# Seven block products in place of eight for the FFN output products of a two-layer decoder trunk

## The reference

```python
def swiglu(h, w_in, w_out):
    gu = h @ w_in                              # (512, 1024) @ (1024, 5632)
    g, u = jnp.split(gu, [FFN_HIDDEN], axis=-1)     # FFN_HIDDEN = 2816
    return (jax.nn.silu(g) * u) @ w_out        # (512, 2816) @ (2816, 1024)

    for layer in range(DEPTH):
        ...
        x = x + rms_norm(m, norm_mix_post[layer])
        hn = rms_norm(x, norm_ffn_pre[layer])
        x = x + rms_norm(swiglu(hn, ffn_w_in[layer], ffn_w_out[layer]), norm_ffn_post[layer])
```

## Time and profile before

| what | us |
|---|---|
| median of three runs | 1206.71 |
| span of the profiled execution | 1204.9 |
| TensorE busy | 1193.1 |
| GpSimd (POOL) busy | 517.1 |
| ScalarE (ACT) busy | 398.4 |
| VectorE (DVE) busy | 321.0 |

### The profile page before, as it was taken

The page is one execution under the profiler, slowest core; times in us unless marked ns, Lnnn a source line. Parts: engine busy times, 40 slices in busy tenths (PEclk is TensorE's granted clock), DMA queues, the critical chain, the costliest instruction groups (busy, mean ns, idle before and its releaser), DMA issues.

```text
span 1204.9 us, 14579 instructions
## 1 busy us (share of the span) xinstructions
PE 1193.1 (99%) x5566; PEld 988.6 (82%) x5566; DVE 321.0 (27%) x553; ACT 398.4 (33%) x623; POOL 517.1 (43%) x288
## 2 busy tenths in 40 slices
PE   7999999999999999999999999999999999999998
PEld 6888887898888888888888888788888888888886
DVE  3351056251011111000056835825211111110002
ACT  5112336453233323222243324634433323331210
POOL 4546431744444344444427433033644344435330
PEclk9999999999999999999999999999999999999999
DMA  7454303243232323222443352022332323223211
GB/s 269 128 127 138 105 2 104 72 140 106 87 104 87 104 89 103 92 101 97 159 147 129 98 163 83 18 70 88 106 105 87 104 90 102 94 98 99 94 53 70
DMA packets 34648, 123.82 MB, mean 103 GB/s; under 512 B 3715, under 2 KB 3971, under 8 KB 34348
## 3 DMA queue, kind: packets, MB, share of 16 engines
q1 hardware_dynamic: 30328, 109.94, 27.0%
q10 hardware_dynamic: 4276, 13.26, 3.8%
HBM read 119.76 MB, written 3.42 MB: 102 GB/s over the span
## 4 chain that ended last, share of the span: by engine, by line
PE 99%; DMA 0%; DVE 0%; ACT 0%; DVEq 0%; POOLq 0%; issue 0%; POOL 0%
PE ps L1053 30%; PE ps L1055 30%; PE ps L1054 30%; PE ps L1260 2%; PE ps L1226 2%; PE ps L1083 1%; PE ps L1244 1%; DMA ident<-ident_in 0%; PE ps L1272 0%; PE ps L1362 0%; PE ps L1340 0%; PE ps L1224 0%; PE ps L1352 0%; PE ps L1365 0%; PE ps L1223 0%; PE ps L1378 0%
## 5 line engine op out<-in xcount | busy, mean ns | idle before, releaser
L279 POOL TENSOR_TENSOR w_lo<-w_raw,w_hi 128x1024 fp32r<-128x1024 f32 x199 | 477.0, 2412 | 560.7 <-ACT w_hi L387 559.1
L1053 PE MATMUL ps<-h_hi,w_hi 128*128 128x512 f32 (+1 forms) x1008 | 383.7, 381 | 0.0
L1055 PE MATMUL ps<-h_hi,w_lo 128*128 128x512 f32 (+1 forms) x1008 | 382.3, 379 | 0.0
L1054 PE MATMUL ps<-h_lo,w_hi 128*128 128x512 f32 (+1 forms) x1008 | 382.2, 379 | 0.0
L387 ACT ACTIVATE w_hi<-w_raw 128x1024 fp32r<-128x1024 f32 x200 | 209.4, 1056 | 304.4 <-DMA w_raw<-weights 301.9
L1053 PEld LDWEIGHTS ps<-h_hi,w_hi 128*128 128x128 f32 x1008 | 189.6, 188 | 35.9 <-issue 0.5
L1054 PEld LDWEIGHTS ps<-h_lo,w_hi 128*128 128x128 f32 x1008 | 189.7, 188 | 35.5 <-issue 0.2
L1055 PEld LDWEIGHTS ps<-h_hi,w_lo 128*128 128x128 f32 x1008 | 189.6, 188 | 35.5
L1053 PE MATMUL ps<-w_hi,prod_hi 128*128 128x512 f32 x352 | 137.2, 390 | 0.0
L1055 PE MATMUL ps<-w_hi,prod_lo 128*128 128x512 f32 x352 | 137.0, 389 | 0.0
L1054 PE MATMUL ps<-w_lo,prod_hi 128*128 128x512 f32 x352 | 137.0, 389 | 0.0
(11 more groups left out here) (126 smaller groups left out, 758.2 us busy)
## 6 DMA issues: line engine op xcount, KB each, us to landing
w_raw<-weights SPq DMA_DIRECT2D x200, 512.0 KB, 3.3
x<-x_in SPq DMA_DIRECT2D x4, 512.0 KB, 7.1
gain_post<-norms ACTq DMA_DIRECT2D x4, 512.0 KB, 4.0
gate_w_a<-gate_rows ACTq DMA_DIRECT2D x1, 2048.0 KB, 7.1
minus_f<-forget_rows ACTq DMA_DIRECT2D x1, 2048.0 KB, 11.5
gain_pre<-norms ACTq DMA_DIRECT2D x3, 512.0 KB, 4.2
gate_w_b<-gate_rows ACTq DMA_DIRECT2D x1, 1536.0 KB, 10.7
out<-x SPq DMA_DIRECT2D x3, 512.0 KB, 2.6
```

The costliest lines, as they stand in the source:

```text
L279: nc.gpsimd.tensor_tensor(w_lo[:, c % RING], w_raw[:, c % RING], w_hi[:, c % RING].bitcast(F32), ALU.subtract).then_inc(lo_done, 1)
L1053: mm(to, held[0], moved[0], start=start, stop=False)
L1054: mm(to, held[0], moved[1], start=False, stop=False)
L1055: return mm(to, held[1], moved[0], start=False, stop=stop)
```

## The change

The output product is cut in two by two blocks: tokens in halves of 256, hidden units in halves of 11 tiles, output columns in halves of 512. Strassen's identity (in its form with shared sums) gives the four blocks of the result from seven block products. Three of them take a block of the output weights as it is (`W11`, `W22`, `W21`), four take differences of weights (`T1` to `T4`). A product has six chunks, the sixth of half width, so an FFN's output stage has 42 chunks of 12 (or 6) matmuls.

- **Weight differences ("folds").** During the gate and up stage SyncE loads four weight blocks in six pieces into a buffer `stage`, VectorE makes the four differences there (`fold`), SyncE stores them to a DRAM tensor `fold_t`, from which the ring loads them later. Load and store of a piece stand between the ring's loads on SyncE's queue, which is written out in full instead of a loop.
- **Sides.** VectorE makes sums and differences of the activations (`sides`) for pairs 11 to 21; ScalarE and VectorE split each of the six sides in three pieces (`split`).
- **Merging.** Products that enter several blocks are added by VectorE (`merge`) or accumulated on a bank that holds an earlier product.
- **The boundary after layer 0.** Tiles 0 and 1 are complete after product 5, tile 2 within product 6, tile 3 at its end. GpSimd makes the low parts of V1 and V1+1 ahead of its boundary steps and those of V1+2 and V1+3 between them.
- The low parts of the weights are GpSimd's as before, of half width for a sixth chunk.

```diff
-V1 = FOUT0 + FT
+V1 = FOUT0 + 7 * 6
...
+PRODUCTS = ((False, W11), (True, T2), (True, T1), (True, T3), (False, W22), (True, T4), (False, W21))
+PIECES = ((0, 4), (4, 8), (8, FH))
+FOLDS = 6
...
-            groups = N_CHUNKS // RING
-            with nc.sync.Fori(1, groups) as g:
-                for i in range(RING):
-
-                    sp.wait_ge(chunk_used, g * RING + (i + 1 - RING))
-                    sp.dma_start(w_raw[:, i], weights[g * RING + i]).then_inc(raw_landed[i], 16)
...
+            for c in range(AHEAD, N_CHUNKS):
+                if c >= RING:
+                    sp.wait_ge(chunk_used, c + 1 - RING)
+                at = fout(c)
...
+                    if folded_t:
+                        sp.wait_ge(fold_stored, 16 * FOLDS * (layer + 1))
...
+                sp.dma_start(w_raw[:, c % RING, 0:width(c)], source).then_inc(raw_landed[c % RING], 16)
+                for layer in range(2):
+                    j, late = divmod(c - FINS[layer] - 6, 4)
+                    if 0 <= j < FOLDS and late in (0, 2):
+                        part = slice(j * CHUNK, min((j + 1) * CHUNK, FH * SEQ))
+                        held = stage[:, :, 0:part.stop - part.start]
+                        if late == 0:
+
+                            if FOLDS * layer + j:
+                                sp.wait_ge(fold_stored, 16 * (FOLDS * layer + j))
+                            sp.dma_start(held, fold_w[layer].rearrange("b p k -> p b k")[:, :, part]).then_inc(fold_landed, 16)
+                        else:
+                            sp.wait_ge(folded, FOLDS * layer + j + 1)
+                            sp.dma_start(fold_t.ap()[layer].rearrange("b p k -> p b k")[:, :, part], held).then_inc(fold_stored, 16)
...
                 for t in range(1, TILES):
+                    if b == 2 and t <= 2:
+                        low(AFTER[b] + t + 1)
                     post_rstds(b, t)
                     pre_rstds(b, t)
...
+            for c in range(FOUT0 + 6, V1 + 2):
+                low(c)
+            boundary(2)
...
+                act.wait_ge(sides_done, FH * (layer + 1))
+                act.wait_ge(chunk_used, c0)
+                split(0)
+                highs(c0 + 6, c0 + 8)
+                split(1)
+                highs(c0 + 8, c0 + 12)
+                act.wait_ge(chunk_used, c0 + 6)
...
+                split(2)
+                highs(c0 + 12, c0 + 18)
+                split(3)
+                highs(c0 + 18, c0 + 24)
+                act.wait_ge(chunk_used, c0 + 12)
+                split(4)
+                split(5)
+                highs(c0 + 24, c0 + 32)
...
+            act.wait_ge(chunk_used, FOUT0 + 36)
             act.dma_start(gate_w[0][:], gate_rows[0:4].partition_broadcast(P)).then_inc(gate_w_landed[0], 16)
...
+            def fold(layer, j):
+
+                n = min(CHUNK, FH * SEQ - j * CHUNK)
+                w11, w12, w21, w22 = (stage[:, i, 0:n] for i in range(4))
+                vec.wait_ge(fold_landed, 16 * (FOLDS * layer + j + 1))
+                own(nc.vector.tensor_tensor(w11, w12, w11, ALU.subtract))
+                nc.vector.tensor_tensor(w12, w22, w12, ALU.subtract)
+                own(nc.vector.tensor_tensor(w22, w22, w11, ALU.subtract))
+                nc.vector.tensor_tensor(w21, w21, w22, ALU.subtract).then_inc(folded, 1)
...
+                nc.vector.tensor_tensor(s1, a21, a22, ALU.add)
+                own(nc.vector.tensor_tensor(a21, a11, a21, ALU.subtract))
+                own(nc.vector.tensor_tensor(a11, s1, a11, ALU.subtract))
+                nc.vector.tensor_tensor(s4, a12, a11, ALU.subtract).then_inc(sides_done, 1)
...
+                for p in range(FT):
+                    if p % 2 == 0 and p // 2 < FOLDS:
+                        fold(layer, p // 2)
+                    if p == FH:
+
+                        vec.wait_ge(fold_stored, 16 * FOLDS * (layer + 1))
+                    vec.wait_ge(silu_done, tile0 + p + 1)
...
+                def split(n):
+                    raw, hi, lo = SIDES[n]
+                    for i, (k0, k1) in enumerate(PIECES):
+                        vec.wait_ge(side_hi, len(PIECES) * (len(SIDES) * layer + n) + i + 1)
+                        nc.vector.tensor_tensor(lo[:, k0:k1, :], raw[:, k0:k1, :], hi[:, k0:k1, :].bitcast(F32),
+                                                ALU.subtract).then_inc(side_ready, 1)
...
+                product(0, (4, 6), False, first_ready)
+                product(1, (0, 2), False, side(0))
+                pe.wait_ge(product_done, FT * (layer + 1))
+                product(2, (5, 7), False, side(1))
...
+                for i in range(3):
+                    chunk(6, i, (4, 6), True, side(5)).then_inc(chunk_used, 1)
+                for t in range(2):
+                    if b < 4:
+                        turn(b, t)
+                    for i in range(3, 6):
+                        last = chunk(6, i, (4, 6), True, side(5), (t,))
```

More of the change, by code:

```diff
@@ L365, in _ @@
                 nc.gpsimd.tensor_tensor(y, y, ret_gate[:, :, h * HEAD:(h + 1) * HEAD], ALU.mult).then_inc(ret_y, 1)
-            at = OUT0 + 3
-            for b in range(1, 4):
-                lows(at, AFTER[b] + AHEAD - 1)
-                boundary(b)
-                at = AFTER[b] + AHEAD
-            lows(at, N_CHUNKS)
+            lows(OUT0 + 3, AFTER[1] + AHEAD - 1)
+            boundary(1)
+            lows(FIN0 + AHEAD, FOUT0)
+            lows(FOUT0, FOUT0 + 6)
+            for c in range(FOUT0 + 6, V1 + 2):
+                low(c)
+            boundary(2)
+            lows(V1 + AHEAD, AFTER[3] + AHEAD - 1)
+            boundary(3)
+            lows(FIN1 + AHEAD, FOUT1)
+            lows(FOUT1, FOUT1 + 6)
+            for c in range(FOUT1 + 6, N_CHUNKS):
+                low(c)
             boundary(4)
@@ L696, in own, with half_scale @@
                 vec.wait_ge(vec_step, steps[0])
-            def half_scale(b):
-                for t in range(TILES):
+            def half_scale(b, tiles=range(TILES)):
+                for t in tiles:
+                    bank = half_bank(b, t)
                     vec.wait_ge(half_summed, 4 * (b - 1) + t + 1)
@@ new lines, in halves_of, with ffn_out, split, merge @@
+            def halves_of(row, n=SEQ):
+                return row.rearrange("p (a s) -> p a s", s=n)
+            def ffn_out(layer):
+                c0, b = FOUTS[layer], 2 * layer + 2
+                def split(n):
+                    raw, hi, lo = SIDES[n]
+                    for i, (k0, k1) in enumerate(PIECES):
+                        vec.wait_ge(side_hi, len(PIECES) * (len(SIDES) * layer + n) + i + 1)
+                        nc.vector.tensor_tensor(lo[:, k0:k1, :], raw[:, k0:k1, :], hi[:, k0:k1, :].bitcast(F32),
+                                                ALU.subtract).then_inc(side_ready, 1)
+                def merge(to, bank, held):
+                    nc.vector.tensor_tensor(to, ps[:, bank, :], held, ALU.add).then_inc(merged, 1)
+                split(0)
+                split(1)
+                split(2)
+                for t in range(2):
+                    vec.wait_ge(chunk_used, c0 + 12)
+                    vec.wait_ge(first_copied, 2 * layer + t + 1)
+                    merge(work[:, t, :], 2 * t, work[:, t, :])
+                split(3)
+                for t in range(2):
+                    vec.wait_ge(chunk_used, c0 + 18)
+                    vec.wait_ge(merged, 10 * layer + t + 1)
+                    merge(work[:, 2 + t, :], 5 + 2 * t, work[:, t, :])
+                split(4)
+                split(5)
+                for t in range(2):
+                    vec.wait_ge(chunk_used, c0 + 24)
+                    vec.wait_ge(merged, 10 * layer + 2 + t + 1)
+                    merge(ps[:, 1 + 2 * t, :], 2 * t, work[:, 2 + t, :])
+                half_scale(b, (0, 1))
+                for t in range(2):
+                    vec.wait_ge(chunk_used, c0 + 30)
+                    merge(ps[:, 5 + 2 * t, :], 5 + 2 * t, work[:, t, :])
+                half_scale(b, (2, 3))
+                for t in range(2):
+                    vec.wait_ge(chunk_used, c0 + 36)
+                    merge(ps[:, 2 * t, :], 2 * t, work[:, t, :])
@@ L941, in _ @@
             boundary(1)
[L942 removed]
+            ffn(0)
+            ffn_out(0)
             boundary(2)
[L945 to L946 removed]
             def dots(n0, n1):
```

292 lines of the change are left out of this document (186 added, 106 removed).

## The result

The changed kernel takes 1214.1 us, median of four runs (1212.3 to 1215.2); the kernel before, on the same chip, 1206.8. The ratio is 1.006, with an interval of 1.0048 to 1.0072: slower by 7.3 us, by 0.6%. The forecast of 1206.9 was 7.2 us too low; the time lies between its own upper end (1212) and the slower rival (1227), in the interval that the prediction gave to folds that are too slow (above 1212, chance 0.33). The profiled execution of the changed kernel is the fastest of the four: 1212.3 us, span 1210.4, 5.5 more than the span before.

A forecast was written before the change was run, and what follows sets the result against it. TensorE, busy 99% of the span, was taken as the bound. From 1206.7 us, -29.9 (matmuls) + 4.8 (low parts) + 13.5 (end of layer 0) + 11.8 (folds) = +0.2: 1206.9, own range 1202 to 1212, eight in ten 1185 to 1230.

The forecast's parts named there:

- Matmuls: Output products of both layers: 462 instead of 528 matmuls a layer, at 0.226 us each, 29.9 us less.
- Low parts late: Output products: GpSimd, taking turns with VectorE, reaches product 4's first chunk late; TensorE waits 2.4 us a layer, 4.8 together.
- E: End of a layer's up products, the zero from which the prediction counted times in the output stage.
- End of layer 0: Layer 0's last output products: TensorE waits 9.7 us to turn tile 0 and 3.8 for tile 1, together 13.5.
- Folds: Gate and up stages: late weight differences hold up TensorE, 5.9 us a layer, 11.8 together, range 0 to 32.
- The clock: Gate and up stages: the first fold's 3.8 us wait may end in slow matmuls, 1.0 us (0 to 2.5).
- The pauses for the product: Gate and up stages: TensorE waits 3.8 us at the first fold, 1.0 at the second, 0 to 0.5 at later ones.
- Port costs little: GpSimd hardly held up, differences hidden, only 8.6 us at layer 0's end stay: 1185 us; chance with a halfway case 0.32.
- Folds don't fit the period: Gate and up stages: slow transfers of 6.2 us make a 24.2 us cycle, some 16 us a layer: 1227; chance 0.33.
- It doesn't do what it says: Rival doubting the matmul saving; dismissed because seven products with the same 512 columns are fewer matmuls; no chance given.
- Covers costed at nothing: Gate-row loads, VectorE's wait for the last store, merges and copies: each expected to cost nothing.

The follow-up runs named there:

- without splits: Changed kernel without VectorE's subtractions for the low parts of the six sides, TensorE passing the high part twice, as many matmuls: 1206.6 us, ratio to before 1.0003.
- half folds: Changed kernel with the weight differences made in eleven pieces of 512 columns instead of six of 1024, alternating between two buffer halves: 1196.4 us, ratio to before 0.9916.
- the kernel with one buffer: Against the kernel with half-size pieces in two buffer halves: every piece goes through the same half, each load waiting for the store before it: 1247.4 us.

## Why the prediction was nearly right, and where it fell short

- **Matmuls**, -29.9: measured 15.0 in layer 1 (119.5 against 104.5 without splits), taken to be the same in layer 0.
- **Low parts late**, 2.4 a layer: measured 2.5 in layer 1 (107.0 against 104.5), where nothing else disturbs. TensorE's longest pause in these products came at 560.4 in layer 0, 60.3 us after E (500.1), where E+59.8 was forecast. Up to there 15 split operations stood beside the low parts, at 0.9 us each, where the sum had a dozen at 1.1: 13 us either way. The price of a turn was about right too: five low parts with four full operations among them took 16.07 us, 4.2 more than 5 x 2.37, 1.05 an operation. That is less than the 1.21 that the operation takes alone, and the half-size ones of the half folds cost less again (13.91 us for the same five low parts). The Trainium skill ("SBUF — State Buffer", section "SBUF: two separate sides") has the pair held for the whole instruction; the trace agrees on the turns and shows a little less than the whole.
- **End of layer 0**, 13.5: the waits are 12.4. GpSimd was done with V1+1 at 604.0, E+103.9, where E+104 was forecast, and TensorE stood there at 600.3, E+100.2, where it was E+100.3. The first wait is 1.9 longer than the 9.7 forecast, since VectorE's last step waited for V1+2's low part, a meeting that the step left out; the second is shorter (0.8 instead of 3.8), because TensorE came to it later: its work after the first turn ran at half clock.
- **Folds**, 11.8: measured 16.1. The waits for the product are 9.4 in the list, against 9.8 forecast (3.8, 1.0 and little a layer). The differences ended at 271.9, where 275.3 was forecast (1.0 of it is the earlier start of the stage; most of the rest, that the first of them didn't wait for a low part), and store and load took longer, 7.5 and 8.0 where 6.4 and 7.1 were worked out. That the two errors nearly cancel is luck.
- **The mis-sized terms.** The losses come to 36.4 us where the sum had 30.1. *The clock*: half clock behind the first fold stood in the sum with 1.0 a layer; it took 1.6 and 2.8, 2.4 more in all. *The pauses for the product*: counted from matmul to matmul, with those too short for the list, they are 11.7 where the list has 9.4 and the forecast had 9.8, 1.9 more. *The end of layer 0*: without the low parts 15.3 against 13.5, 1.8 more, which is VectorE's last step beside a low part. The low parts add 0.2. The half clock at the end of layer 0, which the sum had at nothing, cost no time of its own as far as the trace shows: tile 1's row came at E+119.9 from GpSimd and VectorE, 7.8 us after tile 0's, and TensorE, slow or not, waited for it. The profiled execution comes to +5.5 with its earlier start, and the median lies another 1.8 above that execution. The first wait of a gate and up stage, whose instructions are the same in both, was 2.7 us in the changed kernel and 4.9 without splits; this spread would explain the wider one of the runs (2.9 us against 0.2 before), but no run here singles it out.
- **The rivals.** *Port costs little*: no; fold operations take 3.3 us beside running low parts, and a run without splits is 7.5 faster. *Folds don't fit the period*: right in its mechanism, a chain longer than its period, and right in the length of the transfers: with its 6.2 us for the bytes a load comes to 8.2 and a store to 7.5, and 8.0 and 7.5 were measured. Its reason for them was wrong: the DMAs moved 419 and 416 GB/s in full stretches, above the 408 of the earlier trace rows, with the weight loads beside the fold's own. Its cycle was too long as well: 7.5 + 8.0 + 7.0 = 22.5 at the second fold instead of 24.2, so the later waits stayed at 0.2 to 0.7, where it had 2.5 a fold, and didn't grow. Alone the transfers cost nothing. The Trainium skill's 358 GB/s to HBM ("SBUF — State Buffer", section "A bandwidth-pool intuition that's wrong") is exceeded by these windows as by that row. *It doesn't do what it says*: it does.
- **Covers costed at nothing** held: the gate rows, the last store's wait, merges and copies don't appear in the list of waits.
- **Two slips** of 0.2 in the working change nothing: 4 x 14.9 is 59.6, and 4.6 + 2 is 6.6.

## What to carry to other kernels

When TensorE is busy for 99% of the span, work that is taken off it must be paid for by engines that until then had slack: list what they do in the new, shorter period, engine by engine, and treat any chain of load, compute and store through one buffer as a bound of its own, to be compared with its period. Here such a chain, 26.9 and 28.6 us long where it began beside a run of low parts and some 22.5 after that, against a period of 21.7, cost 18 us, and two half buffers brought all of it back at the same work. And the two long waits of TensorE in these stages cost more than half of their length again (2.7 and 1.6, 4.8 and 2.8 us), because the clock came back late.

## What the runs showed of the hardware that was not expected

- TensorE's clock after a pause, counted from matmul to matmul: of 2.7 us, 3.2 us of work at 0.5; of 4.8 us (layer 1's first fold), 5.7; of 12.0 us, 8.5 us of 0.5 while it still waited and 5.0 of work. The length alone doesn't settle it: in the kernel with one buffer a pause of 2.7 us (at 349.8) was followed by work at 1.00. After the pause of 1.6 us as the fifth product begins the clock stayed at 1.00:

```profile
558.00:564.00 6.00, 4.78 (x22) 3.65 (x21) 5.92 (x4) 2.44 (x3) 6.00 (x3) 1.00 0.60 169
```

- VectorE and GpSimd take turns by instruction even when both have several queued, so an operation of 0.69 us takes 2.8 and one of 1.21 takes 3.3 beside a run of low parts. A VectorE operation with one input in PSUM wasn't held up: the product at 271.81 takes 0.67 beside the five low parts.
- A store of 2.1 MB to DRAM took 7.5 us and a load of as much 8.0, the weight loads beside them included; a half piece 5.0 and 5.3.
